# One block for the whole first transformer block: waits at first use in place of barriers between phases

## The reference

```
h = rms_norm(x, norm1_g);  z = h @ w_in + b_in          # split into columns
y_ml  = rms_norm(mlstm(mq, mk, mv, mi, mf)) * sigmoid(mo)
y_fx  = forgetting_attention(rms_norm(fq), rms_norm(fk), fv, ff)
y_lru = scan(conv1d(rx), sigmoid gates wa, wx) * gelu(ry)
y_gla = rms_norm(gla(gq, gk, gv, log_alpha)) * silu(gg)
x = x + (sum_n sigmoid(gates_n) * (y_n @ w_branch_n)) @ w_o
x = x + relu(rms_norm(x) @ w_up)**2 @ w_down
```

## Time and profile before

| | |
|---|---|
| median of 3 runs | 3513.57 us (3513.09 to 3514.7) |
| profiled execution | 3513.62 us, its span 3511.4 us |
| PE busy | 3339.7 us (95%) |
| DVE, ACT, POOL busy | 1528.1, 1284.4, 321.9 us (44%, 37%, 9%) |
| granted clock of PE, mean | 0.974 |

### The profile page before, as it was taken

How to read it: one execution, slowest core, us unless ns; L and a number is a source line. 1 busy time by engine, 2 the same in 40 slices (tenths; PEclk the granted TensorE clock), 3 DMA queues, 4 the chain that set the end, 5 groups by cost and what they waited for, 6 DMA issues and landing times. The chain is left out here.

```text
span 3511.4 us, 37516 instructions
## 1 busy us (share of the span) xinstructions
PE 3339.7 (95%) x14912; PEld 2656.2 (76%) x14912; DVE 1528.1 (44%) x2423; ACT 1284.4 (37%) x2212; POOL 321.9 (9%) x148
## 2 busy tenths in 40 slices
PE   7999899999999999999988999999999999899998
PEld 6766677877888888876676788878887667678886
DVE  4153522135343333344786533343334378563334
ACT  3344633234232322234465422232223336742222
POOL 0411324410000000003200000000000230000000
PEclk9998999999999999999999999999999999999999
DMA  4211222322333333322101233323333310023332
GB/s 135 92 40 36 77 63 90 96 89 86 101 96 98 96 96 96 96 99 84 31 1 38 89 98 99 96 82 100 96 90 105 96 54 1 13 72 102 96 96 72
DMA packets 77069, 280.60 MB, mean 80 GB/s; under 512 B 8800, under 2 KB 9056, under 8 KB 76640
## 3 DMA queue, kind: packets, MB, share of 16 engines
q1 hardware_dynamic: 76896, 278.21, 26.0%
HBM read 276.08 MB, written 2.10 MB: 79 GB/s over the span
## 5 line engine op out<-in xcount | busy, mean ns | idle before, releaser
L520 ACT ACTIVATE w_hi<-raw_slabs 128x1024 fp32r<-128x1024 f32 x496 | 524.2, 1057 | 1320.5 <-PE ps L560 1150.9
L535 DVE TENSOR_TENSOR w_lo<-raw_slabs,w_hi 128x1024 fp32r<-128x1024 f32 x372 | 455.1, 1224 | 747.7 <-ACT w_hi L520 747.6
L560 PE MATMUL ps<-in_hi,w_hi 128*128 128x512 f32 x1840 | 720.6, 392 | 15.0 <-DVE in_lo L877 8.3
L560 PE MATMUL ps<-in_lo,w_hi 128*128 128x512 f32 x1840 | 718.3, 390 | 0.0
L560 PE MATMUL ps<-in_hi,w_lo 128*128 128x512 f32 x1840 | 717.9, 390 | 0.0
L560 PE MATMUL ps<-parts,w_hi 128*128 128x512 f32 x2240 | 693.0, 391 | 7.7 <-PEq L384 7.7
L535 POOL TENSOR_TENSOR w_lo<-raw_slabs,w_hi 128x1024 fp32r<-128x1024 f32 x124 | 305.7, 2466 | 2567.1 <-ACT w_hi L520 2567.1
L560 PEld LDWEIGHTS ps<-parts,w_hi 128*128 128x128 f32 x2240 | 421.5, 188 | 97.4 <-issue 10.0
L560 PE MATMUL ps<-parts,w_lo 128*128 128x512 f32 x1120 | 436.5, 390 | 0.0
L560 PEld LDWEIGHTS ps<-in_hi,w_hi 128*128 128x128 f32 x1840 | 346.6, 188 | 93.7 <-issue 15.7
L560 PEld LDWEIGHTS ps<-in_hi,w_lo 128*128 128x128 f32 x1840 | 346.9, 189 | 72.5
(11 more groups left out here) (270 smaller groups left out, 3492.7 us busy)
## 6 DMA issues: line engine op xcount, KB each, us to landing
raw_slabs<-weights SPq DMA_DIRECT2D x510, 512.0 KB, 3.6
big<-rope SPq DMA_DIRECT2D x2, 2304.0 KB, 8.8
x_resid<-xT SPq DMA_DIRECT2D x8, 256.0 KB, 5.1
outT<-x_resid SPq DMA_DIRECT2D x8, 256.0 KB, 2.0
const_cols<-consts SPq DMA_DIRECT2D x1, 836.0 KB, 9.1
scratch<-brow SPq DMA_DIRECT2D x1, 768.0 KB, 9.5
vector_cols<-vec SPq DMA_DIRECT2D x2, 45.5 KB, 9.4
vector_cols<-vec SPq DMA_DIRECT2D x1, 69.0 KB, 4.0
```

What stands on the lines that cost most here:

```text
L520: self.nc.scalar.activation(self.w_hi[:, m % SPLIT, :], self.raw[:, n % RAW, :], ACT.Copy)\
L535: (self.nc.gpsimd if i is None else self.nc.vector).tensor_tensor(self.w_lo[:, m % SPLIT, :], self.raw[:, n % RAW, :], self.w_hi[:, m % SP ...
L560: mm = k.nc.tensor.matmul(out, lhsT, rhs, start=(c == 0 and m == 0), stop=(last and m == 2))
```

## The change

All phases of the first block are put under one `k.together()`, so that the barriers between them go. Each place at which an engine first uses something that another engine made or freed in an earlier phase gets a wait of its own (`k.now(flag, less)`: the flag's count at that point, less some). Banks are chosen so that a phase starts on banks that have been free for long. Queries and keys come head by head; the norm of the last key group moves from the end of the mLSTM phase into the attention (`LastNorm`: its sums before unit 2's scores, its root on ACT after unit 1's exponential, its scaling on DVE after unit 1's maximum). In the linear attention all steps come one job later, and the turn of the keys comes after job 0 instead of before it. `split_phase` is removed: the halving of merged tile d moves into the merging (`high`, `low`), and the projection waits for each tile's low half (`Halved`).

```diff
-    w["fq"] = one("w_in", 0, KD, FQ, 4)
-    w["fk"] = one("w_in", 0, KD, FK, 4)
+    w["fq"], w["fk"] = zip(*[[s.columns("w_in", 0, KD, [(0, col + P * j, P)]) for col in (FQ, FK)] for j in range(4)])
...
+    def now(self, name, less=0):
+        return self.flag(name), self.base[name] - less
...
 gemm_phase:
+                for signal in after.get(j, ()) if after else ():
+                    pe.wait_ge(*signal)
...
+                for signal in job.get("over", ()):
+                    act.wait_ge(*signal)
...
 merge_phase:
+                if j == 1:
+                    pe.wait_ge(*sums_taken)
...
+                       (lambda pe, c: pe.wait_ge(halves_ready[0], halves_ready[1] + 4 * j + c + 1)) if j < 3 else None)
...
+            def high(d):
+                act.wait_ge(merged, k.at(merged, 3 * d + 3))
+                nc.scalar.activation(out_parts(d)[0], out(d), ACT.Copy).then_inc(hi_ready, 1)
+
             for j in range(n_jobs):
+                if j >= 4 and j % 3 == 1:
+                    high(j // 3 - 1)
...
+            high(KD - 1)
...
+            def low(d):
+                dve.wait_ge(hi_ready, k.at(hi_ready, d + 1))
+                nc.vector.tensor_tensor(out_parts(d)[1], out(d), out_parts(d)[0].bitcast(F32), ALU.subtract)\
+                    .then_inc(lo_ready, 1)
+
+            dve.wait_ge(*product_ready)
             for j in range(n_jobs):
+                if j >= 4 and j % 3 == 2:
+                    low(d - 1)
...
+            low(KD - 1)
...
+class Halved:
+    def tensor(self, pe):
+        for signal in self.banks_free:
+            pe.wait_ge(*signal)
+
+    def wait_tile(self, pe, c):
+        pe.wait_ge(self.lo, self.before + c + 1)
...
 Mlstm:
         if j < 0:
+            pe.wait_ge(*self.gates_ready)
...
         if j == 0:
+            pe.wait_ge(*self.keys_ready)
...
-        if j == 7:
-            self.norm_sums(pe)
...
-        if j == 7:
-            self.norm.root(act, j)
...
-        if j == 7:
-            self.norm.scaled(dve, j)
...
+class LastNorm:
+    BANK, UNIT = 7, 1
+    def tensor(self, pe, i):
+        k, norm = self.norm.k, self.norm
+        if i == 0:
+            for signal in self.banks_free:
+                pe.wait_ge(*signal)
+        if i % QB == 0:
+            pe.wait_ge(norm.normed, k.at(norm.normed, 2 * (i // QB) + 2))
+        if i == self.UNIT + 1:
+            pe.wait_ge(*self.evicted)
+            norm.bank = self.BANK
+            norm.sums(pe, self.g)
+            pe.wait_ge(norm.logged, k.at(norm.logged, self.g))
+
+    def scalar(self, act, i):
+        if i == self.UNIT:
+            self.norm.root(act, self.g)
+
+    def vector(self, dve, i):
+        if i == self.UNIT:
+            self.norm.scaled(dve, self.g)
...
 Gla:
-    FIRST, EACH = 2, 2
-    ROOTS = 11
+    FIRST, EACH = 3, 2
+    ROOTS = 12
...
-        if j < 0:
+        if j == 0:
+            pe.wait_ge(*self.banks_free)
+            pe.wait_ge(*self.gates_ready)
             self.turn(pe)
-        if j == 0:
+            pe.wait_ge(s["lo_ready"], self.at("lo_ready", 4))
+        if j == 1:
             self.add_states(pe)
-            pe.wait_ge(s["lo_ready"], self.at("lo_ready", 4))
...
 block_one:
-    gemm_phase(k, jobs, scalar={2: gates.scalar}, vector=masks_and_gates)
+    gemm_phase(k, jobs, scalar={2: gates.scalar}, vector=masks_and_gates, bank=4, banks=4, after={0: [k.now("taken", 4)]})
...
+               bank=6, banks=2, after={j: [k.now("taken")] for j in range(2)},
+               between=Mlstm(k, tile(28), tile(32), value(0), lambda h: y(0, h), norm, k.now("m_sum"), k.now("taken", 4)))
+    lead = LastNorm(norm, k.now("taken"), [k.now("head_done"), k.now("abs_den"), k.now("weighted")])
...
+                                     lambda h: y(1, h), P ** -0.5, extra=less_f), lead=lead, first=1)
...
+               ... banks=4, after={0: [k.now("laid"), k.now("probs_expd")]},
+               between=NormBehind(norm, k.now("stored")))
...
+                   for j in range(4)], bank=4, banks=4,
+               after={j: [(conv_step, done + 4 * (j + 1)), k.now("norm_logged")] for j in range(4)})
...
+               vector=beside, after={0: [k.now("taken", 8)], 4: [k.now("taken")]})
...
+    gemm_phase(k, jobs, bank=2, banks=2, after={0: [k.now("taken", 6)], 1: [k.now("taken", 6)]}, between=Gla(
...
-    split_phase(k, [(merged(d), *merged_parts(d)) for d in range(KD)])
-    with k.together():
...
 build:
-        block_one(k, x, const, brow, vec1, vec2)
+        with k.together():
+            block_one(k, x, const, brow, vec1, vec2)
```

More of the change, by code:

```diff
@@ L592, in tiles_of, with gemm_phase @@
     return [i for _, i, *_ in job["sum"] if i is not None]
-def gemm_phase(k, jobs, norm=None, scalar=None, vector=None, banks=None, bank=0, between=None):
+def gemm_phase(k, jobs, norm=None, scalar=None, vector=None, banks=None, bank=0, between=None, after=None):
     nc = k.nc
@@ L1407, in project_phase, with merge_phase @@
         norm.passed()
-def merge_phase(k, tiles, y_parts, out):
+def merge_phase(k, tiles, y_parts, out, out_parts, sums_taken, halves_ready, product_ready):
     nc = k.nc
     ends = k.use([r for g, b in tiles for r in (range(g, g + KD), range(b, b + 4))])
-    gate, merged, product = [k.flag(n) for n in ("gate_ready", "merged", "gated_product")]
+    gate, merged, product, hi_ready, lo_ready = [k.flag(n) for n in (
+        "gate_ready", "merged", "gated_product", "hi_ready", "lo_ready")]
     n_jobs = len(tiles)
@@ L1461, in _, with __init__, scalar, vector @@
             k.low_slabs(pool)
-    k.passed(gate_ready=n_jobs, gated_product=n_jobs, merged=n_jobs)
+    k.passed(gate_ready=n_jobs, gated_product=n_jobs, merged=n_jobs, hi_ready=KD, lo_ready=KD)
+class Halved:
+    def __init__(self, lo, before, banks_free):
+        self.lo, self.before, self.banks_free = lo, before, banks_free
+    def tensor(self, pe):
[3 more added lines that the diff above has]
+        pe.wait_ge(self.lo, self.before + c + 1)
+    def scalar(self, act, ahead=None):
+        pass
+    def vector(self, dve, ahead=None):
+        pass
+    def passed(self):
+        pass
 class MlstmGates:
@@ L1803, in lay_and_store, with attention_phase @@
         nc.scalar.activation(one.out, k.ps[lo:hi, 5 + one.group % 3, 0:P], ACT.Copy).then_inc(stored, 1)
-def attention_phase(k, units, index=None, steps=range(0)):
+def attention_phase(k, units, index=None, steps=range(0), lead=None, first=0):
     nc = k.nc
@@ L1815, in attention_phase @@
     probs = lambda i: k.scr[:, i % ring, :]
+    bank = lambda i: (first + i) % 3
     col = lambda kind, i: k.stat[:, kind, i:i + 1]
@@ L1826, in _ @@
                         pe.wait_ge(expd, k.at(expd, i - 2))
-                    score(k, units[i], i % 3).then_inc(scored, 1)
+                    if lead:
+                        lead.tensor(pe, i)
+                    score(k, units[i], bank(i)).then_inc(scored, 1)
                 attend(k, pe, i - lag, n, units, probs, probs_ready, turned, laid, unit_done, stored)
@@ L2011, in scalar_gates @@
         _, r, _, _, u, _, _ = self.tiles
+        act.wait_ge(*self.ready)
         act.wait_ge(s["lam_ready"], k.at(s["lam_ready"], 1))
@@ L2039, in vector @@
         xc, r, i, ygate, u, sq, y = self.tiles
+        dve.wait_ge(*self.ready)
         for j in range(4):
@@ L2135, with __init__ @@
     BANKS = (0, 1, 4, 5)
-    FIRST, EACH = 2, 2
-    ROOTS = 11
-    def __init__(self, k, gates, q, v, states, y, norm, halves, sums, out, taken):
+    FIRST, EACH = 3, 2
+    ROOTS = 12
+    def __init__(self, k, gates, q, v, states, y, norm, halves, sums, out, taken, banks_free):
+        self.banks_free, self.gates_ready = banks_free, k.now("q_scaled")
+        self.exps_done = k.now("back_exp")
         self.k, self.gates, self.q, self.v, self.states, self.y = k, gates, q, v, states, y
@@ L2226, in scalar @@
         if j < 0:
+            act.wait_ge(*self.exps_done)
+        if j == 0:
             for p in range(2):
@@ L2703, in block_one @@
     y = lambda n, c: big[:, 12 + 4 * n + c, :]
-    with k.together():
[L2705 to L2713, removed]
+    norm = ResidNorm(k, "norm1_g", eps="rms_eps", out=k.act)
+    later = [(k.const[:, NORM_CONST:], const[:, NORM_CONST:]),
+             (scr[:, 9:12, :], brow.rearrange("a (b c) -> a b c", c=T).broadcast_to([P, 3, T])),
+             *[(k.vec[:, VEC1.n + l * VEC2.n:VEC1.n + (l + 1) * VEC2.n], vec2[l]) for l in range(LAYERS)]]
+    here, count = copy_in_phase(k, x_in, [(k.const[:, 0:NORM_CONST], const[:, 0:NORM_CONST]),
+                                          (k.vec[:, 0:VEC1.n], vec1)], later, norm)
+    token_phase(k, act, [(w[key], lambda tb, n=n: big[:, 4 * n + tb, :], scr[:, 9 + n, :])
+                         for n, key in enumerate(("mv", "fv", "gv"))], norm, bias_here=(here, k.at(here, count)))
+    k.passed(inputs_here=count, norm_here=32)
     jobs = []
@@ L2766, in block_one @@
```

(2 more changed lines are left out.)

84 lines of the change are left out of this document (39 added, 45 removed).

## The result

The changed kernel takes 3478.91 us (median of 4, 3475.98 to 3481.45) against 3513.33 us (median of 4, 3509.19 to 3514.7) for the kernel before on the same chip: a ratio of 0.9909, 95% interval 0.9896 to 0.9923, so 34.4 us (1.0%) faster. The forecast was 3463, a gain of 50.9; the measured time is outside its likeliest span (3457 to 3469) and just inside the wide one (3456 to 3480). The profiled execution took 3477.99 us, its span 3476.2.

The account below looks back on a forecast made before the run. PE was taken to lose time at the first block's barriers, in waits and the clock's falls behind them. Boundary gains of 4.5 + 1.0 + 20.2 + 0.6 + 0.9 + 0 + 7.4 + 7.5 + 8.8 = 50.9 gave 3463 us, range 3456 to 3480.

Parts of the forecast that it names:

- these five boundaries: First block to features 4.5, features to mLSTM 1.0, attention to rx/ry 0.6, rx/ry to small gates 0.9, then features 0.
- with PE hardly pausing I take it that the clock stays up: Attention start: without the 5.64 us nearly idle, PE keeps full clock; if not, only 4.8 us are left.
- rival (a): Attention: clock falls there all the same, for all or part; costs up to 15.4 us, 3466 to 3478; chance 0.27.
- The 20.2: mLSTM to attention: gain in us, unit 10 starting at about 283.6 and not at 303.75.
- 17.9 of its second working: Attention, first score to tenth unit's end: 34.45 us busy at grant 0.52 is 17.9 at full clock.
- Features to linear attention: First merging gate, 5.5 us, covers the 4.54 us wait; gain 4.54 + 2.9 = 7.4 us.
- this price (about 2 us): Linear attention to merging: without the barrier DVE and POOL may exclude each other, making the sum about 2 us smaller.
- Linear attention to merging: A 5.5 us gate covers the halving; 6.65 + 3.1 saved, less 2.2 for a late slab: gain 7.5 us.
- merging to projection: Halving moves into the merging; 7.70 us of barriers and split_phase goes, a 1.0 wait stays: gain 8.8 us.
- Rival (b): Three long barriers hid work; 7.4 + 7.5 + 8.8 shrinks by half or more: 3475 to 3490; chance 0.11.
- Rival (c): Merging: halving inside it stops PE; the change turns slower at 5.3 us for each of eight rounds; chance 0.02.
- Later stages are unchanged.: After the first block: the same 510 slabs in the same order, SP loading never later; no gain or loss counted.

Follow-up runs that it names:

- pair 1: First profiles of the kernel before and of the changed kernel, compared at equal matmul counts; spans 3511.4 and 3476.2 us, lead 35.2.
- pair 2: Later profiles of the same two unchanged kernels, compared at equal matmul counts; spans 3501.7 and 3473.1 us, lead 28.6.
- POOL held: Changed kernel with POOL waiting for DVE's four differences before halving its slab ahead of the linear attention; 3468.9 us, 0.9887 of the kernel before.

## Why the prediction was right and where it was wrong

**First block, mLSTM, rx/ry, small gates.** Right: forecast 7.0 for these five boundaries, measured 8.5 in pair 1 (4.7 + 1.1 + 0.9 + 1.6 + 0.2) and 5.8 in pair 2 (3.1 + 1.1 + 0.9 + 1.5 - 0.8). The difference at the first is that the kernel before had its 3.4 us at half in one profile and not in the other. The slab wait of 2.97, expected at 4.0, is 3.02 with 0.5 ahead of it.

**mLSTM to attention.** The order was as worked out: sums without a wait, first turn 7.1 us after the first score (forecast 7.0), PE without a gap. The step that failed is "with PE hardly pausing I take it that the clock stays up". PE didn't pause, and the clock fell all the same in three of six profiles, which was rival (a) at 0.27. The 20.2 was the size with no fall (20.3 measured), and of the kernel before's longest fall. With the changed kernel's fall of 17.1 it is 12.5. That it came so close is in part luck: 2.5 heads of 9.55 less 3.6 are 20.3 and not the 19.4 of the prediction, and the 19.1 that it goes on with is neither that nor the 17.9 of its second working. Both kernels vary here from execution to execution, so the term is a spread of some 8 to 20 and not a number: the 8 (35.56 - 27.73) is the pairing that no pair showed. The rival's range, 3466 to 3478, was still short of 3479, since the other two misses come on top. The argument against (a), that the same mix had held 1.00 for 19.83 us, took one execution for a property of the code. The banks are cycled in the same way in the executions with and without the fall, so the rule of the Trainium skill cited there (TensorE: Matmul & The Clock Gate, section "A second HAM failure mode: psum-queue depth-cycling") decides nothing between them.

**Features to linear attention.** The mechanism held, the cover was mis-sized. ACT and DVE "needed 4.5 to finish" in the kernel before. There the barrier kept the second slab behind it, and only the first of the four differences met it:
```profile
433.77 2.34 POOL L535 TENSOR_TENSOR w_lo<-raw_slabs,w_hi 128x1024 fp32r<-128x1024 f32 x1 [8.10 <-ACT w_hi L520]
437.97 2.38 POOL L535 TENSOR_TENSOR w_lo<-raw_slabs,w_hi 128x1024 fp32r<-128x1024 f32 x1 [1.85 <-ACT w_hi L520]
440.00 2.70 DVE L2259 TENSOR_TENSOR parts<-big,parts 128x512 fp32r<-128x512 f32 x4 [2.84 <-ACT parts L2222]
```
Without the barrier POOL halves two slabs back to back just as the differences come, one difference stands for 2.8 us, and PE waits 3.35, with the clock at half behind it: 2.5 instead of 7.4. The prediction had this rule and this price (about 2 us), but looked for it one boundary later. With POOL held 6.1 are gained (2.5 and 3.6); the rest is the 1.21 that PE still waits.

**Linear attention to merging, merging to projection.** Right, 8.6 and 8.0 for 7.5, 8.8 and 8.6 for 8.8. The slab comes late 13 us into the merging and costs 1.81 (forecast 2.2), the projection waits 0.84 (forecast 1.0):
```profile
520.96 0.50 PE L563 MATMUL ps<-in_hi,w_hi 128*128 128x512 f32 x1 [1.81 <-POOL w_lo L538]
```
```profile
707.05 0.74 PE L563 MATMUL ps<-parts,w_hi 128*128 128x512 f32 x2 [0.84 <-DVE scratch L1464]
```
Rival (b), barriers that hid work, is out for these two and half true for the one above. Rival (c) is out: no wait in the merging names the halving.

**"Later stages are unchanged."** The work is; its time isn't. This sentence costed 2600 us of code at nothing, and it was worth -7.8 and -8.7. The forecast's allowance, 6 us either way for falls at another place, was made for the first block alone.

In sum for pair 1: 50.9 forecast; -7.7 at the attention, -4.9 at the linear attention, -8.7 behind the projection (0.9 and 7.8), +2.6 at the other boundaries, +3.0 from what isn't the change (1.3 by which the first products start earlier, 1.7 for a fall inside the mLSTM): 35.2. In pair 2 the three misses are -4.3, -4.7 and -9.8.

## What to carry to other kernels

When a barrier goes, list what ran alone behind it: an engine that the barrier kept still may now run beside the one that the next stage waits for, and stretch it. Before a stretch at low clock is booked as gain, look at it in two executions of the same kernel; here it was 34 or 24 us in one kernel and 17 or 0 in the other. A lead won early shifts all that follows against the chip's clock control, as the layers show, so compare the unchanged part too, stretch by stretch at the same count of matmuls.

## What the runs showed of the hardware

The granted clock fell in a stretch in which PE was busy throughout (264.07 to 281.14) and stayed at 1.00 in the same stretch of the same program in another execution. A VectorE difference with two inputs in SBUF that met a GpSimd difference ended 0.54 to 0.55 us after it, in all three cases among the sixteen of the changed kernel: 2.83 and 0.87 to 0.89 us instead of 0.68. Delaying PE by 1.15 us ahead of the layers took 8.9 us off two stretches of them; delaying it by 2.3 took nothing off.
